# Third layer's mixer: gated heads one unit later, six gates of the second branch first, one sigmoid per gate

## The reference, cut to what matters

```
proj = rmsnorm_2(h, norm_mix_w) @ w_in      # u, q k v r a_lr (gla), q k v (diff), gates
y_a = s5_branch(u, ...)                     # complex scan over time, then gelu(y) @ w_glu
y_b = gla_branch(q, k, v, r, a_lr, ...)     # 4 gated heads, chunks of 32 positions, rms norm, @ gla_w_br
y_c = diff_attn_branch(q, k, v, ...)        # 4 heads of differential attention, rms norm, @ diff_w_br
g = sigmoid(gates).reshape(bsz, seq, 3, D_MODEL)
merged = g[:, :, 0] * y_a + g[:, :, 1] * y_b + g[:, :, 2] * y_c
h = h + merged @ w_out
```

## Time and profile before

| what | value |
|---|---|
| median of 3 runs | 3158.02 us (3157.24 to 3164.36) |
| the profiled execution, its own time | 3157.95 us |
| its span | 3156.2 us |
| TensorE busy | 3074.1 us (97%) |
| VectorE busy | 2307.6 us (73%) |
| ScalarE busy | 1841.5 us (58%) |
| GpSimd busy | 534.1 us (17%) |
| TensorE's share of the chain that ended last | 82% |
| DMA engines, mean rate | 178 GB/s |

### The profile page before, as it was taken

How to read it: one execution, slowest core, us unless ns; L and a number is a source line. 1 busy time by engine, 2 the same in 40 slices (tenths; PEclk the granted TensorE clock), 3 DMA queues, 4 the chain that set the end, 5 groups by cost and what they waited for, 6 DMA issues and landing times.

```text
span 3156.2 us, 53599 instructions
## 1 busy us (share of the span) xinstructions
PE 3074.1 (97%) x21726; PEld 2842.8 (90%) x21726; DVE 2307.6 (73%) x3156; ACT 1841.5 (58%) x2373; POOL 534.1 (17%) x640
## 2 busy tenths in 40 slices
PE   7999999999999999999999999999999999999997
PEld 6889998889999999888888889999998888888886
DVE  6655888657788877676866887876666888887544
ACT  5554788645766777554664554445445666666443
POOL 2000000000000000116735556750001000000000
PEclk9999999999999999999999999999999999999999
DMA  5445444556555566565433445556555555555554
GB/s 202 153 154 178 151 155 172 187 188 216 182 186 181 179 188 206 193 201 187 161 121 120 155 140 174 174 170 211 187 184 190 188 192 189 190 191 189 191 188 139
DMA packets 158473, 560.50 MB, mean 178 GB/s; under 512 B 17600, under 2 KB 25856, under 8 KB 157712
## 3 DMA queue, kind: packets, MB, share of 16 engines
q1 hardware_dynamic: 158224, 557.06, 53.0%
HBM read 550.64 MB, written 6.36 MB: 176 GB/s over the span
## 4 chain that ended last, share of the span: by engine, by line
PE 82%; DVE 9%; ACT 6%; issue 2%; POOL 1%; DMA 0%; SPq 0%; DVEq 0%; ACTq 0%; POOLq 0%
PE ps L566 81%; DVE WL L1342 2%; ACT WH L913 2%; ACT L903 2%; DVE XC L1316 0%; POOL PB L1942 0%; DVE XMC L1316 0%; DMA RAW<-in_w 0%; DVE XC L1332 0%; DVE BX L1305 0%; POOL PT L1942 0%; DVE BS L1305 0%; DVE IB L1305 0%; POOL TB L1942 0%; ACT RS L903 0%
## 5 line engine op out<-in xcount | busy, mean ns | idle before, releaser
L566 PE MATMUL ps<-XN,WH 128*128 128x256 f32 (+1 forms) x8864 | 1851.7, 302 | 27.0 <-DVE XN L1316 17.9
L913 ACT ACTIVATE WH<-RAW 128x1024 fp32r<-128x1024 f32 x1010 | 1064.8, 1057 | 1114.6 <-PE ps L566 1078.9
L1342 DVE TENSOR_TENSOR WL<-RAW,WH 128x1024 fp32r<-128x1024 f32 x1010 | 1262.3, 1257 | 482.0 <-ACT WH L913 474.1
L566 PEld LDWEIGHTS ps<-XN,WH 128*128 128x128 f32 x8864 | 1431.8, 192 | 104.0 <-DVE XN L1316 18.9
L566 PE MATMUL ps<-XN,WL 128*128 128x256 f32 x5120 | 1443.4, 282 | 0.0
L566 PEld LDWEIGHTS ps<-XN,WL 128*128 128x128 f32 x5120 | 979.4, 191 | 0.0
L566 PE MATMUL ps<-YS,WH 128*128 128x512 f32 (+1 forms) x1088 | 371.3, 388 | 7.3 <-DVE YS L1305 3.8
L566 PE MATMUL ps<-YS,WL 128*128 128x256 f32 x1056 | 296.4, 281 | 0.0
L1942 POOL TENSOR_TENSOR RSB<-RSB,SQ 128x256 f32<-128x256 f32 x75 | 76.3, 1017 | 1224.1 <-ACT SQ L903 1222.9
L566 PEld LDWEIGHTS ps<-YS,WH 128*128 128x128 f32 x1088 | 203.5, 189 | 52.0 <-DVE WL L1342 4.4
L566 PE MATMUL ps<-HS,WH 128*128 128x512 f32 x688 | 238.6, 392 | 0.0
(11 more groups left out here) (332 smaller groups left out, 3330.2 us busy)
## 6 DMA issues: line engine op xcount, KB each, us to landing
RAW<-in_w SPq DMA_DIRECT2D x1010, 512.0 KB, 3.3
CSB<-sums SPq DMA_DIRECT2D x64, 128.0 KB, 3.7
X<-scratch SPq DMA_DIRECT2D x2, 2048.0 KB, 8.1
X<-in_x SPq DMA_DIRECT2D x4, 512.0 KB, 7.9
X<-in_x SPq DMA_DIRECT2D x1, 2048.0 KB, 8.0
scratch<-X SPq DMA_DIRECT2D x1, 2048.0 KB, 8.6
scratch<-X SPq DMA_DIRECT2D x4, 512.0 KB, 5.4
out<-X SPq DMA_DIRECT2D x4, 512.0 KB, 2.6
```

Source lines behind the costliest of these rows:

```text
L566: return pe.e.matmul(dst, l, r, start=start, stop=stop, skip_group_check=True)
L913: act.e.activation(WH[:, w % NH, :], RAW[:, w % NB, :], ACT.Copy).then_inc(*act.one(("wh", w)))
L1342: dve.e.tensor_tensor(WL[:, w % NB, :], RAW[:, w % NB, :], WH[:, w % NH, :].bitcast(F32), SUB).then_inc(*dve.one(("wl", w)))
```

## The change

Three things. First, in each gated head everything from the product of keys and queries on comes one step, that is one unit, later; the s5 pairs do too (they begin at step 9 + 12 m). Steps 0 of gla (the scaling of q and k), all of dec and all evacuations of the streamed products stay where they are. The bank of a head's output stays out of the ring until step 19 (before 16), that of an attention head until 15 (before 13). Second, the order of the gates: the gates of the second branch (c = 0) for n = 0 to 5 come first, with their `gb` products between, then those of the third branch for n = 0 to 5 with `db`; from n = 6 on the order is as before. The last steps of gla head 3 and of diff heads 2 and 3 are forced later. Third, every gate has a sigmoid of its own, with four slots given out in the new order; two waits of VectorE's DQ evacuation are gone, and it waits for `do` of head 3 before `gb` 4 instead.

```diff
+GATES = [(n, 0) for n in range(6)] + [(n, 1) for n in range(6)] + [(n, c) for n in range(6, 16) for c in range(2)]
+SLOT = {g: i % 4 for i, g in enumerate(GATES)}
...
         if h == 0:
-            p += [End("gla", (2,)), End("gla", (3,)), End("lam", ()), Now("dbl", ())]
-        elif h > 1:
+            p += [End("gla", (2,)), End("lam", ()), Now("dbl", ())]
+        elif h == 1:
+            p.append(End("gla", (3,)))
+        else:
             p.append(End("diff", (h - 2,)))
         p.append(Go("diff", (h,)))
-    p.append(End("diff", (2,)))
-    for m in range(0, 16, 2):
-        for n in (m, m + 1):
-            for c in range(2):
-                p.append(whole(tile("g12", (n, c), "w_in_2", 7184 + 2048 * (c + 1) + 128 * n), 16))
-        for n in (m, m + 1):
-            p.append(whole(tile("gb", (n,), "gla_w_br_2", 128 * n, "gos"), 8))
-        if m == 0:
-            p.append(End("diff", (3,)))
-        for n in (m, m + 1):
-            p.append(whole(tile("db", (n,), "diff_w_br_2", 128 * n, "dos"), 8))
+    for n, c in GATES:
+        p.append(whole(tile("g12", (n, c), "w_in_2", 7184 + 2048 * (c + 1) + 128 * n), 16))
+        if (n, c) == (5, 0):
+            p += [gb(4), gb(5), End("diff", (2,)), End("diff", (3,))]
+        elif (n, c) in ((1, 0), (3, 0)):
+            p += [gb(n - 1), gb(n)]
+        elif (n, c) in ((1, 1), (3, 1), (5, 1)):
+            p += [db(n - 1), db(n)]
+        elif n > 5 and n % 2 and c:
+            p += [gb(n - 1), gb(n), db(n - 1), db(n)]
...
-                if s == 2:
+                if s == 3:
                     b = take("side", "gs", h)
...
-                if 5 <= s <= 8:
-                    p = s - 5
+                if 6 <= s <= 9:
+                    p = s - 6
                     b = take("side", "kv", h, p)
...
-                if s == 11:
+                if s == 12:
                     b = take("side", "go", h)
...
-                if s == 16:
+                if s == 19:
                     kept.discard(holder_of("go", h))
-                if s == 14:
+                if s == 15:
                     b = take("side", "gn", h)
...
-                if s == 13:
+                if s == 15:
                     kept.discard(holder_of("do", h))
...
-                rms_tail(h, s - 12, "go", "gn", GOS, OB, "g")
+                rms_tail(h, s - 13, "go", "gn", GOS, OB, "g")
...
             def g12(n, c, s):
-                if s == 1 and c == 1:
-                    act.wait_ge(*at("sgr", n, 1))
-                    sl = SG[:, 2 * (n % 2):2 * (n % 2) + 2, :]
-                    fn(sl, sl, ACT.Sigmoid, ("sg", n))
+                if s == 1:
+                    act.wait_ge(*at("sgr", n, c))
+                    fn(SG[:, SLOT[n, c], :], SG[:, SLOT[n, c], :], ACT.Sigmoid, ("sg", n, c))
...
-    return [(m, s - 8 - 12 * m) for m in range(16) if 0 <= s - 8 - 12 * m < 13]
+    return [(m, s - 9 - 12 * m) for m in range(16) if 0 <= s - 9 - 12 * m < 13]
```

More of the change, by code:

```diff
@@ L72, in whole, with gb, db @@
     return Part(t, list(range(kt)), True, True)
+GATES = [(n, 0) for n in range(6)] + [(n, 1) for n in range(6)] + [(n, c) for n in range(6, 16) for c in range(2)]
+SLOT = {g: i % 4 for i, g in enumerate(GATES)}
+def gb(n):
+    return whole(tile("gb", (n,), "gla_w_br_2", 128 * n, "gos"), 8)
+def db(n):
+    return whole(tile("db", (n,), "diff_w_br_2", 128 * n, "dos"), 8)
 def plan():
@@ L1174, in gla @@
                     fn(GR[h % 2], GR[h % 2], ACT.Silu, ("grs", h))
-                if s == 3:
+                if s == 4:
                     act.wait_ge(*at("gs", h))
@@ L1227, in s5 @@
                         fn(BS[i][:, 1, :], b[:, 0:256], ACT.Copy, ("bx", n), ("free", "bu", n), scale=-1.0)
-                if s == 202:
+                if s == 203:
                     act.wait_ge(*at("usd", 7))
                     fn(US, US, ACT.Gelu_apprx_tanh, ("gelu",))
-                if s == 204:
+                if s == 205:
                     fn(ZS[:, :, 0:256], US, ACT.Copy, ("zsh",))
             def g12(n, c, s):
-                if s == 1 and c == 1:
-                    act.wait_ge(*at("sgr", n, 1))
-                    sl = SG[:, 2 * (n % 2):2 * (n % 2) + 2, :]
-                    fn(sl, sl, ACT.Sigmoid, ("sg", n))
+                if s == 1:
+                    act.wait_ge(*at("sgr", n, c))
+                    fn(SG[:, SLOT[n, c], :], SG[:, SLOT[n, c], :], ACT.Sigmoid, ("sg", n, c))
             def g0(n, s):
@@ L1740, in gla @@
                     tt(GE2, k_, GE2, MUL, ("ge2", h))
-                if s == 4:
+                if s == 5:
                     dve.wait_ge(*at("ktm", h))
@@ L1746, in gla @@
                        ("free", "gs", h))
-                if 6 <= s <= 9:
-                    p = s - 6
+                if 7 <= s <= 10:
+                    p = s - 7
                     dve.wait_ge(*at("kv", h, p))
@@ L1757, in gla @@
                                 ("free", "kv", h, p))
-                rms_tail(h, s - 12, "go", lambda j: cv("gla_norm", j), GOS, OB, GR[h % 2], "g")
+                rms_tail(h, s - 13, "go", lambda j: cv("gla_norm", j), GOS, OB, GR[h % 2], "g")
             def rms_tail(h, s, bo, w, OS, ob, by, key):
@@ L1786, in dq @@
                     dve.wait_ge(*at("ds", h - 2, 1))
-                if j == 0 and h == 1:
-                    dve.wait_ge(*at("gosh", 3))
-                    dve.wait_ge(*at("go", 3))
                 evac(DQ[h % 2][:, j, :], 2, "dq", h, j, more=[("dqd", h, j)])
@@ L1838, in s5 @@
                             ("free", "sy", ft))
-                if s == 206:
+                if s == 207:
                     dve.wait_ge(*at("zsh"))
@@ L1847, in g12 @@
                     dve.wait_ge(*at("ds", 2, 1))
-                if n > 1:
-                    dve.wait_ge(*at("sg", n - 2))
-                evac(SG[:, 2 * (n % 2) + c, :], 2, "g12", n, c, more=[("sgr", n, c)])
+                evac(SG[:, SLOT[n, c], :], 2, "g12", n, c, more=[("sgr", n, c)])
             def gb(n, s):
                 dve.wait_ge(*at("tile", "gb", n))
-                dve.wait_ge(*at("sg", n))
-                tt(PSM[:, n, :], bank("gb", n)[:, 0:256], SG[:, 2 * (n % 2), :], MUL, ("free", "gb", n))
+                dve.wait_ge(*at("sg", n, 0))
+                if n == 4:
+                    dve.wait_ge(*at("do", 3))
+                tt(PSM[:, n, :], bank("gb", n)[:, 0:256], SG[:, SLOT[n, 0], :], MUL, ("free", "gb", n))
             def db(n, s):
@@ L1860, in db @@
                 dve.wait_ge(*at("tile", "db", n))
-                tt(VB[:, n % 2, :], bank("db", n)[:, 0:256], SG[:, 2 * (n % 2) + 1, :], MUL, ("free", "db", n))
+                dve.wait_ge(*at("sg", n, 1))
+                tt(VB[:, n % 2, :], bank("db", n)[:, 0:256], SG[:, SLOT[n, 1], :], MUL, ("free", "db", n))
                 tt(PSM[:, n, :], PSM[:, n, :], VB[:, n % 2, :], ADD, ("ydn", n))
```

## The result

| | before | after |
|---|---|---|
| median of 22 runs each | 3159.65 us (3156.11 to 3166.03) | 3165.86 us (3164.09 to 3171.16) |
| the profiled execution | 3157.95 us | 3165.16 us |
| its span | 3156.2 us | 3163.4 us |
| TensorE's waits, 1480 to 1900 us | 22.9 us | 27.4 us |
| half clock, 1450 to 2100 us | 13.7 us in 4 stretches | 27.3 us in 5 |

The ratio is 1.0019 [1.0013, 1.0024]: 6 us slower, within the 0.3% that the prediction calls the same, though the interval doesn't contain 1. The forecast was 3161.6 us, the range 3149 to 3172. Waits and half clock are read from one profiled execution per kernel, the medians from all its executions. One execution of all, the profiled one of experiment 6, ran at a mean granted clock of 0.75 and took 3737.77 us; its time and its trace are left out.

The account below looks back on a forecast made before the run. TensorE, busy 3074.1 of 3156.2 us, bounds the kernel, with 22.9 us of waits in the changed stretch. Terms sum to +2.7 us of waits and +0.9 of clock: 3158.02 + 2.7 + 0.9 = 3161.6 us, range 3149 to 3172.

Parts of the forecast that it names:

- start of s5: First s5 pair: TensorE's US wait (1.9 us) and a small wait of the first sy (0.4) go: -2.3 us.
- heads 1 and 3: GE's waits (3.4 us) go, but KTM delays the gate's logarithm: stalls of 4.0 at sy, 4.8 with lam; net +5.4.
- sum of waits: TensorE's waits, 1480 to 1900 us, total about 25 us; under 18 would mean the VectorE chain is wrong.
- kv behind BX: kv's second product waits for a bank ScalarE empties behind gv (dv): 4.8 us in heads 0/1, 3.1 in 2/3.
- kv behind the norm: kv's last product waits for gn's Ln and Exp with two table loads: 0.9 us, twice.
- bu behind DS: Diff head 0: s5's bu waits for ds's bank, emptied by VectorE behind DQ, US and OB: 3.6 us.
- SQ, DOS gone: Diff heads 2 and 3, no longer pushed through at once: waits for SQ (2.5) and DOS (1.4) go, -3.9 us.
- dw of head 3 behind RS: Diff tail: dw of head 3 waits for head 2's dnm Ln and Exp, behind a sigmoid with table load: +2.3 us.
- rival 1: VectorE keeps up, so sy and lam don't wait in heads 1 and 3: 8.8 us less waiting, 3149.4 us; chance 0.15.
- Rival 2: Gate stretch: sy starts to wait, up to 1 us at each of seven places: 3168.6 us; chance 0.12.
- a half drop more: Mixer stretch: one clock drop per 5.7 us of waiting gives 4.5 drops now, half a drop more: +0.9 us.
- Rival 3: Each wait of over 3 us drops the clock: eight drops instead of four, 3167.5 us; chance 0.13.

Follow-up runs that it names:

- experiment 6: Changed kernel with sigmoids last in their unit on ScalarE and diff's steps first on VectorE: 3160.71 us, ratio 1.0004 to before.
- experiment 4: Changed kernel with ScalarE's gv and dv evacuations behind its other work of their unit: 3159.45 us, ratio 0.9995 to before.
- experiment 3: Changed kernel with s5's second product (sy) one unit later, at step 11 instead of 10: 3153.34 us, ratio 0.9980 to before.
- experiment 5: Kernel of experiment 4 with ScalarE's dec also ahead of its gla in the same unit: 3168.59 us, ratio 1.0030 to before.
- experiment 1: Kernel before with the gate part alone (new gate order, a sigmoid each, later end of diff 2 and 3), no shift: 3156.3 us, ratio 0.9990.
- experiment 11: Changed kernel with only ScalarE's sigmoids last in their unit: 3160.51 us, ratio 1.0001 to before.
- experiment 10: Kernel of experiment 7 with VectorE's two small lam operations first in their unit: 3141.72 us, ratio 0.9941 to before.
- experiment 7: Changed kernel with the edits of experiment 3, experiment 4 and experiment 6 together: 3142.93 us, ratio 0.9948 to before.
- experiment 9: Kernel of experiment 1 (heads and s5 not shifted) with the orders of experiment 7, sy late included: 3152.09 us, ratio 0.9977 to before.
- experiment 2: Changed kernel with the gate part undone, so only heads and s5 go a unit later: 3167.2 us, ratio 1.0024 to before.
- experiment 12: Kernel before with twelve TensorE waits put into the feed-forward part, each for four POOL additions: 3247.96 us (two executions).

## Why the prediction was right, and where it was not

The time came within the range and on the forecast's own side, 4.3 us above it: 1.6 because before itself measured 3159.65 and not 3158.02, 1.8 from the waits, and the rest, 0.9, is left to the clock. The mechanism, the same work with fewer but longer waits, is what the traces show. Two of its terms were mis-sized, and one was wrong.

Part of the hit is luck. The start of s5 came out 4.7 us worse than forecast and heads 1 and 3 5.2 us better; these two errors, each larger than the change forecast (3.6), cancel. The sum of waits, which below 18 us was to give a wrong VectorE chain away, was too coarse a sign: that error alone would have left it at 20.4. And the range of 23 us was wide against a change of 3.6.

| step of the prediction | forecast | measured |
|---|---|---|
| start of s5 | -2.3 | +2.4 |
| heads 1 and 3: sy and lam | 4.0, 4.8 | 1.7, 1.9 |
| GE's waits gone | -3.4 | -3.4 |
| kv behind BX | 4.8, 3.1 | 4.95, 3.24 |
| kv behind the norm | 0.9, 0.9 | 1.0, 1.0 |
| OB's 3.5 gone | yes | yes |
| bu behind DS | 3.6 | 3.8 |
| SQ, DOS gone | -3.9 | -3.9 |
| dw of head 3 behind RS | 2.3 | 2.9 |
| smaller waits left | 1.2 | 1.9 |
| sigmoids, waits after 1900 | 0 | 0 |
| waits, 1480 to 1900 | 25.6 | 27.4 |

**The step that failed: the start of s5.** "Won: 1.9, and 0.4 (of the small waits) for the first sy: -2.3." The US wait did go, though by less than the 3.6 us of air forecast: the last US evacuation ends at 1480.74, and TensorE comes for the bank at 1480.99. But the sy wait did not go: it grew from 0.4 to 2.9, and 1.9 for the second sy came with it. I had shifted VectorE's chain by a unit along with TensorE's. For the first pair it isn't set by the unit but by POOL's TB, after which VectorE starts at 1474.3 and 1474.45 in the two kernels; I had read that very row and used it only for the US evacuation behind it. TensorE gains the US wait and the half clock behind it, is at sy sooner, and pays there. The second pair's wait is mostly gv ahead of BX on ScalarE (experiment 4: 1.9 to 0.6), a stacking that I had counted for kv and not for sy. Experiment 3 confirms that TensorE asked too early: sy a unit later, and all three BS waits are gone.

**Heads 1 and 3: the chain was too long.** 18.3 us from the logarithm to BS were forecast, 16.0 measured (from 1562.2 to 1578.1). The order of the work was right, and so was the place of the stalls, but for head 3, where only lam waits and not the sy behind it; experiment 5 shows that KTM in front of the logarithm is the cause. But it was added up from four stretches of before, and these carry what VectorE's operations took just there. The three operations behind the logarithm, before and after (a stretch of each kernel), and then GE's:

```profile
1559.42:1562.01 2.59, 2.59 (x21) 2.48 (x20) 2.52 (x4) 2.38 (x3) 2.37 (x4) 1.00 0.53 158
```

```profile
1562.19:1563.79 1.60, 1.60 (x15) 1.52 (x13) 1.53 (x4) 1.60 (x2) 0.00 (x0) 1.00 0.00 0
1573.80:1575.15 1.35, 1.35 (x7) 1.13 (x6) 1.28 (x4) 1.06 (x1) 1.18 (x3) 1.00 0.35 55
```

The same three operations took 2.59 us with POOL busy for 2.37, and 1.60 with POOL idle (fifth engine of the row). GE took 1.35 instead of the 2.28 charged; there POOL has records in most of both stretches, so its share isn't shown. These two make 0.99 + 0.93 of the 2.3 us. The DMA share differs in the first pair of rows too (0.53 and 0.00), but it isn't that: between 1450 and 2340 us, in before and after together, all 116 scans of 128x256 that met no record of POOL took 0.69 us, with DMA shares from 0 to 1, and all 20 that met one took 0.92 to 1.12. So 8.8 us of stalls became 3.6. This is half of rival 1 (more air on VectorE), though the stacking did take place.

**kv, gn, bu, dw, the gates.** These are within 0.2 us each, but for dw (2.9 against 2.3, and experiment 1 without the shift has 2.4). They are waits for one named instruction behind a queue that could be written down whole. Rival 2 did not happen: no wait after 1900, and experiment 1 with its 16 sigmoids is not slower. Experiment 11 shows that the sigmoids do cost, but at one place in the diff tail, not in the gate stretch.

**The clock: a half drop more was forecast, 13.7 us more of half clock came.** The rate "one drop per 5.7 us of waiting" was read from waits that were mostly under 2.5 us. A stretch of 3.4 us was also priced a little high, at 1.7: at half clock a 256 wide matmul comes every 0.21 us against 0.120, which loses 1.5. Over these kernels (half clock in one execution each):

| kernel | waits | half clock | median |
|---|---|---|---|
| experiment 10 | 12.7 | 10.2 | 3141.7 |
| experiment 7 | 13.9 | 6.8 | 3142.9 |
| experiment 9 | 16.4 | 17.1 | 3152.1 |
| experiment 3 | 19.2 | 17.1 | 3153.3 |
| experiment 1 | 21.3 | 17.1 | 3156.3 |
| before | 22.9 | 13.7 | 3159.7 to 3160.9 |
| experiment 4 | 23.5 | 20.5 | 3159.5 |
| experiment 11 | 25.6 | 20.5 | 3160.5 |
| after | 27.4 | 27.3 | 3165.9 |
| experiment 5 | 29.1 | 30.7 | 3168.6 |
| experiment 2 | 30.0 | 23.9 | 3167.2 |

A straight line through them rises 1.5 us of time for each us of waiting, with no kernel more than 3.4 us off it. It is drawn after the fact, with before and after among its points (without them it rises 1.5 too). My +2.7 of waits by that rate would have been +4.1; the 4.5 that came give 6.7, and 6.2 were measured. The forecast's 0.9 on top of 2.7 was a rate of 1.3. Rival 3 was near in its effect (3167.5): all four waits of 2.9 us or more from the heads on, 4.9, 3.2, 3.8 and the 2.9 for RS, were followed by a drop, three of them by a double one; the 2.9 at 1492 was followed by none, the 1.9 at 1532 by one. But it had counted each as one 3.4 us stretch. The Trainium skill (TensorE: Matmul & The Clock Gate, HAM oscillation) describes gaps repeated in a loop that drop the clock each time round. Experiment 12 agrees: twelve waits of 4 us, twelve drops.

What stays open: what decides between 0, 3.4 and 6.8 us behind one and the same wait (4.95 us: 6.8 in the changed kernel, 3.4 in experiment 3; 3.5 us in the same code: none in before, 6.8 in experiment 12). Such a choice alone moves the time by 1.5 us or more a place, which bounds what a single step of this kernel can be predicted to, and how much of a few microseconds' difference one profile can explain.

## What to carry to other kernels

When a group of steps is delayed, ask of each chain in it what really sets its time: the unit, or an engine that has its own pace (here POOL's TB). If the producer keeps its own time, the consumer arrives early and waits away what the move gained elsewhere; giving that one consumer (sy) one more unit turned a loss of 6 us into a gain of 6 (experiment 3), and with the orders of experiment 7 the move is worth 9.

Where TensorE is as dense as here, price a microsecond of its waiting above one: 1.5 over these kernels, 1.8 for waits of 4 us. And before an order is swapped, follow the one that loses by it as closely as the one that gains.

## What the runs showed that was not expected

- A wait of about 4 us in otherwise dense work costs nearly twice itself: 49.1 us of such waits made 88 us.
- Half clock comes in steps of 3.4 us (3.4, 6.8, 10.2), and its length isn't a function of the wait alone: 2.9 us of waiting gave 3.4, 3.3 gave nothing, 3.7 gave 6.8.
- VectorE's three operations behind the logarithm took 1.60 us beside an idle POOL and 2.59 beside a busy one; a scan of 128x256 took 0.69 us without POOL and 0.92 to 1.12 with it, whatever the DMA engines did.
- The same code with the same waits had 13.7 us of half clock in two executions and 23.9 in a third.
- Waits of 1.1 to 1.7 us in the dense feed-forward part dropped nothing; in the mixer the 1.9 us for US in the kernel before was followed by a drop.
